# Second projections of the MLP and of the gated stage: half the outputs by seven products of blocks in place of eight

## The chip, the cores and the metric

One core of one Trainium2 chip. The metric is the device time of one execution in microseconds. The core has TensorE (PE, matrix products), VectorE (DVE), ScalarE (ACT), GpSimd (POOL) and SyncE (SP, which here issues the loads).

## The reference

Two decoder blocks run on 256 tokens of width 1024, in float32. The parts that matter here are the feed-forward stages at the end of each block:

```python
h = rmsnorm(x, norm_mlp[layer])
x = x + jnp.square(jax.nn.relu(h @ w_up[layer])) @ w_down[layer]      # w_up 1024x4096, w_down 4096x1024
...
g, u = jnp.split(n @ w_ffn_in, 2, axis=-1)                            # w_ffn_in 1024x5632
return (jax.nn.silu(g) * u) @ w_ffn_out                               # w_ffn_out 2816x1024
```

The rest (two kinds of attention, retention, a state-space mixer, gated linear attention) lies before the MLP, between the two stages, and around them, and the change does not touch it.

## The kernel before

**Numbers in two parts.** Every float32 factor is split in a rounded part `h` (fp32r) and the rest `l`. A product of two such factors is three matmuls, `h h`, `h l` and `l h`. ACT makes `h` by a rounding copy (`round_tile`, L1040), DVE makes `l = raw - h` by a TENSOR_TENSOR with both inputs in SBUF (`rest_of_tile`, L1561).

**Weights.** They come as tiles of 128x1024 (512 KB). SP loads tile i into one of `RAW` = 4 slots (`raws`), once tile i-4 has its `l` (semaphore `lo`, L2391). ACT may round tile i into one of `PARTS` = 5 pairs of slots (`parts`) once TensorE has released tile i-5. The functions `until` and `full` place these roundings and rests, at build time, between the other work of ACT and DVE: before an instruction that waits for a matmul, all those whose slot is released earlier. Each engine then keeps to its order.

**The two stages.** `mlp(u, n, up, w_down)` builds both: u = 0 is the MLP (n = 16 blocks of 256 hidden columns), u = 1 the gated stage (n = 11). Block q of the hidden layer comes from `up(q)`, by `fm`: two tiles and 48 matmuls of 256 columns in the MLP (L374 to L376), four tiles and 96 in the gated stage (`gate` and `prod`). DVE and ACT make it the activated block, in fp32 in `tmps[q % 4]` (MLP: relu on ACT L1300, times itself on DVE L1601; gated: gate scaled on DVE, silu on ACT L1514, product on DVE), and its two parts in `ups[q % 4]` (ACT, then DVE L1595). Then `down(q, 0)` and `down(q, 1)` add the block's share to output columns 0 to 511 and 512 to 1023 of both groups of 128 tokens: one weight tile and 12 matmuls of 512 columns each (L738 to L740). TensorE runs `up(q)`, `down(q-2, 0)`, `down(q-2, 1)`, `up(q+1)` and so on. The four sums stay in four PSUM banks over the stage, and four banks are left for the rest. Some `down(q, 1)` are kept for the end, so that the outputs of columns 0 to 511 can be added to `x` (`residual`), and turned for the next stage, under them.

**GpSimd** computes only small things, the reciprocal roots of the norms, between long waits.

## Time and profile before

| | |
|---|---|
| median of 3 runs | 962.2 us (961.87 to 962.92) |
| profiled execution | 961.55 us, of it span 959.5 us |
| TensorE busy | 952.3 us, 99% |
| VectorE busy | 635.0 us, 66% |
| ScalarE busy | 520.4 us, 54% |
| GpSimd busy | 62.9 us, 7% |
| loads | 170 MB, 178 GB/s in the mean |

The span is the profiled part of an execution. Matmuls overlap in TensorE, so a row's duration is longer than the step from one matmul to the next. What one costs is read from the starts.

### The profile page before, as it was taken

How to read it: one execution, taken by the hardware profiler on the slowest of the kernel's cores; microseconds unless marked ns; L12 is line 12 of the kernel's file. 1: busy time of each engine (PE TensorE's matmuls, PEld its weight loads, DVE VectorE, ACT ScalarE, POOL GpSimd, SP SyncE). 2: the span in 40 equal slices, each digit the busy share in tenths (PEclk: the TensorE clock that was granted, in tenths of full speed). 3: DMA queues.
4: the chain of work that ended last, by engine and by line, in shares of the span. 5: the costliest groups of instructions: out<-in, count | busy, mean ns of one | idle time of the engine just before them, and what ended most of it. 6: DMA issues, size and time to landing. Idle time of an engine off the chain costs nothing.

```text
span 959.5 us, 16218 instructions
## 1 busy us (share of the span) xinstructions
PE 952.3 (99%) x6674; PEld 862.3 (90%) x6674; DVE 635.0 (66%) x826; ACT 520.4 (54%) x788; POOL 62.9 (7%) x112
## 2 busy tenths in 40 slices
PE   9999999999999999999999999999999999999997
PEld 7877889989998888989987999998998899999996
DVE  5768685777555555778867787786666466555545
ACT  5577554555444544666865674545455445444443
POOL 3100001001000000324000001100000010000000
PEclk9999999999999999999999999999999999999999
DMA  9974536556665666556564465555655347565661
GB/s 307 316 231 129 152 88 177 155 176 191 206 196 176 189 185 181 158 181 193 151 198 146 119 180 194 161 191 171 195 163 172 114 154 220 182 202 171 196 192 47
DMA packets 133546, 170.39 MB, mean 178 GB/s; under 512 B 5825, under 2 KB 97297, under 8 KB 133473
## 3 DMA queue, kind: packets, MB, share of 16 engines
q1 hardware_dynamic: 131408, 165.07, 55.7%
q10 hardware_dynamic: 1424, 2.84, 0.9%
q0 software_dynamic: 640, 1.44, 0.6%
q8 instruction: 53, 0.87, 0.4%
q14 instruction: 21, 0.16, 0.1%
HBM read 168.28 MB, written 1.05 MB: 176 GB/s over the span
## 4 chain that ended last, share of the span: by engine, by line
PE 98%; DVE 1%; issue 0%; ACT 0%; POOLq 0%; POOL 0%; ACTq 0%
PE ps L374 15%; PE ps L375 15%; PE ps L376 15%; PE ps L405 8%; PE ps L406 8%; PE ps L407 8%; PE ps L739 5%; PE ps L740 5%; PE ps L738 5%; PE ps L357 4%; PE ps L461 3%; PE ps L494 1%; PE ps L492 1%; PE ps L493 1%; PE ps L627 1%; PE ps L660 1%
## 5 line engine op out<-in xcount | busy, mean ns | idle before, releaser
L1561 DVE TENSOR_TENSOR parts<-raws,parts 128x1024 fp32r<-128x1024 f32 (+2 forms) x307 | 367.3, 1213 | 217.7 <-ACT parts L1040 216.9
L1040 ACT ACTIVATE parts<-raws 128x1024 fp32r<-128x1024 f32 (+2 forms) x307 | 315.5, 1045 | 235.2 <-PE ps L376 133.5
L374 PE MATMUL ps<-room_r,parts 128*128 128x256 f32 x1248 | 351.9, 282 | 0.0
L375 PE MATMUL ps<-room_r,parts 128*128 128x256 f32 x1248 | 348.6, 279 | 0.0
L376 PE MATMUL ps<-room_r,parts 128*128 128x256 f32 x1248 | 348.2, 279 | 0.0
L374 PEld LDWEIGHTS ps<-room_r,parts 128*128 128x128 f32 x1248 | 234.6, 188 | 5.8 <-issue 4.3
L375 PEld LDWEIGHTS ps<-room_r,parts 128*128 128x128 f32 x1248 | 234.7, 188 | 1.3
L376 PEld LDWEIGHTS ps<-room_r,parts 128*128 128x128 f32 x1248 | 234.6, 188 | 0.0
L405 PE MATMUL ps<-parts,room_r 128*128 128x512 f32 (+1 forms) x336 | 133.9, 399 | 0.4 <-DVE parts L1561 0.4
L407 PE MATMUL ps<-parts,room_r 128*128 128x512 f32 (+1 forms) x336 | 131.1, 390 | 0.0
L406 PE MATMUL ps<-parts,room_r 128*128 128x512 f32 (+1 forms) x336 | 131.1, 390 | 0.0
L738 PE MATMUL ps<-parts,room_r 128*128 128x512 f32 x204 | 80.7, 396 | 0.0
L740 PE MATMUL ps<-parts,room_r 128*128 128x512 f32 x204 | 80.7, 396 | 0.0
L739 PE MATMUL ps<-parts,room_r 128*128 128x512 f32 x204 | 80.7, 396 | 0.0
L405 PEld LDWEIGHTS ps<-parts,room_r 128*128 128x128 f32 x336 | 63.1, 188 | 16.1 <-issue 1.7
L407 PEld LDWEIGHTS ps<-parts,room_r 128*128 128x128 f32 x336 | 63.1, 188 | 14.4
L406 PEld LDWEIGHTS ps<-parts,room_r 128*128 128x128 f32 x336 | 63.2, 188 | 13.4 <-issue 0.5
L1595 DVE TENSOR_TENSOR room_r<-room,room_r 128x512 fp32r<-128x512 f32 x47 | 32.5, 692 | 32.5 <-ACT room_r L1305 11.9
L740 PEld LDWEIGHTS ps<-parts,room_r 128*128 128x128 f32 x204 | 38.3, 188 | 9.2
L739 PEld LDWEIGHTS ps<-parts,room_r 128*128 128x128 f32 x204 | 38.3, 188 | 8.2
L738 PEld LDWEIGHTS ps<-parts,room_r 128*128 128x128 f32 x204 | 38.3, 188 | 8.2
L1595 DVE TENSOR_TENSOR room<-room 128x256 f32<-128x256 f32 (+6 forms) x85 | 37.5, 474 | 2.3 <-ACT room L1392 0.7
(225 smaller groups left out, 878.5 us busy)
## 6 DMA issues: line engine op xcount, KB each, us to landing
raws<-in_w_in SPq DMA_DIRECT2D x99, 512.0 KB, 4.5
raws<-in_w_ffn_in SPq DMA_DIRECT2D x44, 512.0 KB, 4.2
raws<-in_w_up SPq DMA_DIRECT2D x32, 512.0 KB, 4.2
raws<-in_w_down SPq DMA_DIRECT2D x32, 512.0 KB, 4.4
raws<-in_w_ffn_out SPq DMA_DIRECT2D x22, 512.0 KB, 4.2
raws<-in_w_xkv SPq DMA_DIRECT2D x16, 512.0 KB, 4.4
raws<-in_w_out SPq DMA_DIRECT2D x8, 512.0 KB, 4.5
raws<-in_w_up_ssd SPq DMA_DIRECT2D x8, 512.0 KB, 5.9
```

Of the source, the lines that this page charges most:

```text
L374: e.matmul(ps, wh, hT[0][:, k, :], start=k == 0, stop=False)
L375: e.matmul(ps, wh, hT[1][:, k, :], start=False, stop=False)
L376: last = e.matmul(ps, wl, hT[0][:, k, :], start=False, stop=k == K - 1)
L405: e.matmul(ps, hT[0][:, k, tok], wh, start=k == 0, stop=False)
L406: e.matmul(ps, hT[0][:, k, tok], wl, start=False, stop=False)
L407: last = e.matmul(ps, hT[1][:, k, tok], wh, start=False, stop=k == K - 1)
L738: e.matmul(ps, uh[:, k, tok], wh, start=q == 0 and k == 0, stop=False)
L739: e.matmul(ps, uh[:, k, tok], wl, start=False, stop=False)
L740: last = e.matmul(ps, ul[:, k, tok], wh, start=False, stop=q == n - 1 and k == 1)
L1040: e.activation(t.h, t.raw, ACT.Copy).then_inc(s["hi"], 1)
L1561: e.tensor_tensor(t.l, t.raw, t.h.bitcast(F32), ALU.subtract).then_inc(s["lo"], 1)
L1595: return e.tensor_tensor(o, i0, i1, op)
```

## The change

Output columns 0 to 511 of both second projections are computed by a scheme of the Strassen and Winograd kind. Per block q, the activations are four blocks of 128x128 (two token groups by two halves of the 256 hidden columns), the weights four blocks of 128x256. Eight block products become seven, each of three matmuls of 256 columns, 21 in place of 12 of 512 columns (`down_by_sums`). They need four sums or differences of the blocks on either side: of the activations (`up_sums_of`, into `u_sums`, 128x512 values) and of the weights (`sums_of`, into `w_sums`, 128x1024 values). GpSimd makes both by three TENSOR_TENSOR each (for the last block DVE makes those of the activations). The weights' sums are a tile of their own in the ring of `parts` (`weight_sums`), which ACT rounds and DVE takes the rest of, so block q has one tile more. Only 768 of 1024 columns of the loaded tile still need that. The activations' sums are rounded by ACT (`sums_rounded`) and have their rest from DVE (`sums_rest`). A raw slot is free once `lo` and the sums are done. At the end the seven products, which lie in four banks, are combined by DVE (`join`). Six banks are now held over the stage, two are left for `up`. In the MLP four `down(q, 1)` are kept for the end, where there were three.

```diff
+            def weight_sums(of):
+                i = len(tiles)
+                h, l = (parts[:, i % PARTS, j, 0:TILE].rearrange("p (k n) -> p k n", k=4) for j in range(2))
+                t = Tile(i, [], 4, 256, chunks(w_sums[len(made) % 2], 4), h, l)
+                t.sums, of.sums = of, t
+                of.raw, of.h, of.l = (v.rearrange("p k (f n) -> p (k f) n", f=2)[:, 1:4, :] for v in (of.raw, of.h, of.l))
+                tiles.append(t)
+                made.append(t)
+                t.nth_sums = len(made)
                 return t
...
-                own = [bank() for _ in range(4)]
+                by_sums = u in (0,1)
+                products = [bank() for _ in range(4)] if by_sums else None
+                own = [None] * 2 * by_sums + [bank() for _ in range(2 if by_sums else 4)]
+                late = 4 if by_sums and u == 0 else 3
+                def product(at, left, right, first, last_):
+                    ps = psum[:, products[at // 2], 256 * (at % 2):256 * (at % 2) + 256]
+                    for (lh, rh), begins, over in (((0, 0), first, False), ((0, 1), False, False), ((1, 0), False, last_)):
+                        last = e.matmul(ps, left[lh], right[rh], start=begins, stop=over)
+                    return last
+                def down_by_sums(q):
+                    need(s["upT"], (16 if u else 0) + q + 1)
+                    w_ = weight(w_down[256 * q:256 * q + 256, 0:512], 2, 512)
+                    sums = weight_sums(w_)
+                    u11, u21, u12, u22 = ([v[:, k, t * P:t * P + P] for v in ups[q % 4]] for k in range(2) for t in range(2))
+                    s3, s1, s2, s4 = ([v[:, i, :] for v in us[q % 4]] for i in range(4))
+                    w11, w22, w21 = ([v[:, i, :] for v in (w_.h, w_.l)] for i in range(3))
+                    t1, t3, t2, t4 = ([v[:, i, :] for v in (sums.h, sums.l)] for i in range(4))
+                    begins, over = q == 0, q == n - 1
+                    need(s["lo"], w_.i + 1)
+                    product(0, u11, w11, begins, False)
+                    last = product(1, u12, w21, False, over)
+                    if over:
+                        ends(last, ("product", u, 0), products[0])
+                    need(s["usT"], nth_us[u] + q + 1)
+                    w_.release = done(product(4, s4, w22, begins, False))
+                    need(s["lo"], sums.i + 1)
+                    product(2, s2, t2, begins, False)
+                    last = product(3, s1, t1, False, over)
+                    if over:
+                        ends(last, ("product", u, 1), products[1])
+                    last = product(5, s3, t3, False, over)
+                    if over:
+                        ends(last, ("product", u, 2), products[2])
+                    last = product(6, u22, t4, begins, over)
+                    if over:
+                        ends(last, ("product", u, 3), products[3])
+                        sums.release = count
+                    else:
+                        sums.release = done(last)
                 def down(q, h):
+                    if by_sums and h == 0:
+                        return down_by_sums(q)
...
                 for q in range(2, n):
                     up(q)
                     down(q - 2, 0)
-                    if q < n - 1:
+                    if q - 2 < n - late:
                         down(q - 2, 1)
                 down(n - 2, 0)
                 down(n - 1, 0)
                 if u:
                     return last_outputs([(q, weight(w_down[256 * q:256 * q + 256, 512:D], 2, 512)) for q in range(n - 3, n)],
                                         own, n)
-                down(n - 3, 1)
+                for q in range(n - late, n - 2):
+                    down(q, 1)
                 if u == 0:
                     where["tail", MIX2] = Group(None, count, None)
                     for t in range(2):
-                        out_of((("down", u), 0, t))
+                        if by_sums:
+                            need(s["joined"], t + 1)
+                        else:
+                            out_of((("down", u), 0, t))
                         turn_x(MIX2, t, 0)
                 down(n - 2, 1)
                 down(n - 1, 1)
...
                 t = tiles[hi]
-                e.wait_ge(landed[t.slot], t.load)
+                if t.nth_sums:
+                    e.wait_ge(s["w_sums"], t.nth_sums)
+                else:
+                    e.wait_ge(landed[t.slot], t.load)
...
+            def sums_rounded(u, q, n):
+                if q == n - 1:
+                    e.wait_ge(s["last_u_sums"], 1 + (u and 1))
+                else:
+                    e.wait_ge(s["u_sums"], nth_us[u] - (u and 1) + q + 1)
+                e.activation(us[q % 4][0], chunks(u_sums[q % 2], 4), ACT.Copy).then_inc(s["us_hi"], 1)
+            def first_copied(u):
+                full(("product", u, 0))
+                e.activation(first_product, psum[:, where["product", u, 0].bank, 0:256], ACT.Copy).then_inc(s["first_product"], 1)
             def up(q):
+                until(where["up", q].at)
+                if q:
+                    sums_rounded(0, q - 1, 16)
                 full(("up", q))
...
+            def up_sums_of(u, q, sem):
+                v, o = tmps[q % 4].rearrange("p k (t n) -> p (k t) n", t=2), chunks(u_sums[q % 2], 4)
+                if nth_us[u] + q >= 2:
+                    e.wait_ge(s["usT"], nth_us[u] + q - 1)
+                step(e.tensor_tensor(o[:, 0:2, :], v[:, 0:4:3, :], bc(v[:, 1, :], 1, [P, 2, P]), ALU.subtract))
+                settle()
+                step(e.tensor_tensor(o[:, 2, :], o[:, 1, :], v[:, 0, :], ALU.add))
+                settle()
+                e.tensor_tensor(o[:, 3, :], o[:, 2, :], v[:, 2, :], ALU.subtract).then_inc(s[sem], 1)
+            def sums_rest(u, q):
+                rest(chunks(u_sums[q % 2], 4), us[q % 4], "us_hi", nth_us[u] + q + 1, "usT")
+            def join(u, factor):
+                p = [psum[:, where["product", u, at // 2].bank, 256 * (at % 2):256 * (at % 2) + 256] for at in range(7)]
+                p37 = chunks(psum[:, where["product", u, 2].bank, :], 2)
+                c = slice(0, 512)
+                until(where["product", u, 3].at)
+                e.wait_ge(s["pe"], where["product", u, 1].at)
+                e.wait_ge(s["first_product"], nth_joint[u] + 1)
+                step(tt(joint[:, 0, :], p[2], first_product, ALU.subtract))
+                settle()
+                emptied(tt(joint[:, 1, :], joint[:, 0, :], p[3], ALU.subtract), ("product", u, 1))
+                emptied(tt(joined[:, 0, 256:512], p[1], first_product, ALU.add), ("product", u, 0))
+                out_of(("product", u, 1))
+                e.wait_ge(s["pe"], where["product", u, 2].at)
+                step(tt(joined[:, :, 0:256], bc(joint[:, 1, :], 1, [P, 2, 256]), p37, ALU.subtract))
+                settle()
+                out_of(("product", u, 0))
+                stt(x[:, 0, c], joined[:, 0, :], factor[0], x[:, 0, c], ALU.mult, ALU.add).then_inc(s["joined"], 1)
+                emptied(tt(joint[:, 1, :], p[5], joint[:, 0, :], ALU.subtract), ("product", u, 2))
+                out_of(("product", u, 2))
+                e.wait_ge(s["pe"], where["product", u, 3].at)
+                emptied(tt(joined[:, 1, 256:512], joint[:, 1, :], p[6], ALU.add), ("product", u, 3))
+                out_of(("product", u, 3))
+                stt(x[:, 1, c], joined[:, 1, :], factor[1], x[:, 1, c], ALU.mult, ALU.add).then_inc(s["joined"], 1)
...
             for q in range(11):
                 r, name = tmps[q % 4], ("gate", q)
+                until(where[name].at)
+                if q:
+                    sums_rest(1, q - 1)
                 full(name)
                 emptied(tt(r, halves(bank_of(name)), rows_of(2), ALU.mult), name)
                 name = ("prod", q)
                 full(name)
                 e.wait_ge(s["gated"], q + 1)
                 emptied(tt(r, halves(bank_of(name)), r, ALU.mult), name)
+                if q == 10:
+                    out_of(name)
+                    up_sums_of(1, q, "last_u_sums")
                 rest(r, ups[q % 4], "up_hi", 16 + q + 1, "upT")
+            sums_rest(1, 10)
...
+            def sums_of(t):
+                raw, o = chunks(raws[:, t.slot, :], 4), t.sums.raw
+                e.wait_ge(landed[t.slot], t.load)
+                if t.sums.nth_sums > 2:
+                    e.wait_ge(s["lo"], made[t.sums.nth_sums - 3].i + 1)
+                step(e.tensor_tensor(o[:, 0:2, :], raw[:, 1:3, :], bc(raw[:, 0, :], 1, [P, 2, 256]), ALU.add))
+                settle()
+                step(e.tensor_tensor(o[:, 2, :], o[:, 0, :], raw[:, 2, :], ALU.add))
+                settle()
+                e.tensor_tensor(o[:, 3, :], o[:, 2, :], raw[:, 3, :], ALU.add).then_inc(s["w_sums"], 1)
+            def sums(u, n, ahead=0):
+                for q in range(ahead):
+                    sums_of(made[nth_us[u] + q].sums)
+                for q in range(n):
+                    if q < n - 1:
+                        name = ("prod" if u else "up", q)
+                        e.wait_ge(taken[where[name].bank], where[name].use)
+                        up_sums_of(u, q, "u_sums")
+                    if q >= ahead:
+                        sums_of(made[nth_us[u] + q].sums)
...
-            for t in tiles:
-                if t.i >= RAW:
-                    before = tiles[t.i - RAW]
-                    e.wait_ge(s["lo"], before.i + 1)
+            for t in loaded:
+                if t.before:
+                    e.wait_ge(s["lo"], t.before.i + 1)
+                    if t.before.sums:
+                        e.wait_ge(s["w_sums"], t.before.sums.nth_sums)
                 for to, v in t.srcs:
                     e.dma_start(to, v).then_inc(landed[t.slot], 16)
```

Place one: VectorE over one block of the gated stage (`parts` are the weights' parts; `room` with `rows_rstd` is the scaled gate; `room` with `s_gated` the product; `room_r` with `s_up_hi` the rest of the activated block). Before:

```order
L1595 TENSOR_TENSOR room<-ps,rows_rstd 128x512 [waits s_pe]
L1561 TENSOR_TENSOR parts<-raws,parts 128x1024 [waits s_hi] x2
L1595 TENSOR_TENSOR room<-ps,room 128x512 [waits s_gated,s_pe]
L1595 TENSOR_TENSOR room_r<-room,room_r 128x512 [waits s_up_hi]
L1561 TENSOR_TENSOR parts<-raws,parts 128x1024 [waits s_hi] x4
```

The same place after, where `s_us_hi` stands for the rounded sums of the activations of the block before:

```order
L1698 TENSOR_TENSOR room_r<-room,room_r 128x512 [waits s_us_hi]
L1698 TENSOR_TENSOR room<-ps,rows_rstd 128x512 [waits s_pe]
L1664 TENSOR_TENSOR parts<-raws,parts 128x1024 [waits s_hi] x2
L1698 TENSOR_TENSOR room<-ps,room 128x512 [waits s_gated,s_pe]
L1698 TENSOR_TENSOR room_r<-room,room_r 128x512 [waits s_up_hi]
L1664 TENSOR_TENSOR parts<-raws,parts 128x1024 [waits s_hi] x3
L1664 TENSOR_TENSOR parts<-raws,parts 128x768 [waits s_hi]
L1664 TENSOR_TENSOR parts<-room,parts 128x1024 [waits s_hi]
```

A rest of 128x512 that waits for GpSimd's sums now stands ahead of the gate, and the rest of the weights' sums (`parts<-room,parts`) behind the loaded tiles.

Place two: GpSimd over one block of the gated stage, none of which was there before (`room<-room` are the activations' sums, those with `raws` the weights'):

```order
L2449 TENSOR_TENSOR room<-raws 128x512 [waits s_lo,s_landed3]
L2451 TENSOR_TENSOR room<-room,raws 128x256 [waits s_pool_step]
L2453 TENSOR_TENSOR room<-room,raws 128x256 [waits s_pool_step]
L2437 TENSOR_TENSOR room<-room 128x256 [waits s_usT,s_taken7]
L2439 TENSOR_TENSOR room<-room 128x128 [waits s_pool_step]
L2441 TENSOR_TENSOR room<-room 128x128 [waits s_pool_step]
```

Each instruction waits for the one ahead of it, and the activations' sums of block q+1 stand behind the weights' sums of block q, whose tile is loaded behind the four tiles of `up(q+2)`.

Place three: ScalarE before the last block of the MLP (`room<-ps` is the relu of that block). Before:

```order
L1040 ACTIVATE parts<-raws 128x1024 [waits s_pe,s_landed3]
L1040 ACTIVATE parts<-raws 128x1024 [waits s_pe,s_landed0]
L1040 ACTIVATE parts<-raws 128x1024 [waits s_pe,s_landed1]
L1040 ACTIVATE parts<-raws 128x1024 [waits s_pe,s_landed2]
L1300 ACTIVATE room<-ps 128x512 [waits s_pe]
L1305 ACTIVATE room_r<-room 128x512 [waits s_taken6,s_pe]
```

After:

```order
L1116 ACTIVATE parts<-raws 128x768 [waits s_pe,s_landed2]
L1116 ACTIVATE parts<-room 128x1024 [waits s_pe,s_w_sums]
L1116 ACTIVATE parts<-raws 128x768 [waits s_pe,s_landed3]
L1116 ACTIVATE parts<-room 128x1024 [waits s_pe,s_w_sums]
L1380 ACTIVATE room_r<-room 128x512 [waits s_u_sums]
L1393 ACTIVATE room<-ps 128x512 [waits s_pe]
L1398 ACTIVATE room_r<-room 128x512 [waits s_taken5,s_pe]
L1380 ACTIVATE room_r<-room 128x512 [waits s_last_u_sums]
```

Two roundings that wait for GpSimd's weight sums, of blocks 13 and 14, now stand ahead of the relu of block 15.

## Rows read from the trace of the kernel before

**Rows 1.** The page: busy time and instructions of engines, TensorE's clock, chain

```profile
PE 952.3 (99%) x6674; PEld 862.3 (90%) x6674; DVE 635.0 (66%) x826; ACT 520.4 (54%) x788; POOL 62.9 (7%) x112
...
PEclk9999999999999999999999999999999999999999
...
PE 98%; DVE 1%; issue 0%; ACT 0%; POOLq 0%; POOL 0%; ACTq 0%
```

**Rows 2.** Waits of TensorE, whole span: us in total, times, longest

```profile
PE ps L357 <- DVE junk L1688: 1.0, 1, 1.0
PE ps L405 <- DVE parts L1561: 0.4, 1, 0.4
```

**Rows 3.** Timeline of TensorE in the MLP: start us, duration us, instruction

```profile
301.12 0.40 PE L740 MATMUL ps<-parts,room_r 128*128 128x512 f32 x1
...
303.92 0.40 PE L740 MATMUL ps<-parts,room_r 128*128 128x512 f32 x1
304.15 0.28 PE L374 MATMUL ps<-room_r,parts 128*128 128x256 f32 x1
...
308.36 0.28 PE L374 MATMUL ps<-room_r,parts 128*128 128x256 f32 x1
```

**Rows 4.** Timeline of VectorE, one block of the MLP (x2: two merged)

```profile
310.85 0.68 DVE L1601 SCALAR_TENSOR_TENSOR room<-ps,room 128x512 f32<-128x512 f32 x1
312.29 0.69 DVE L1595 TENSOR_TENSOR room_r<-room,room_r 128x512 fp32r<-128x512 f32 x1 [0.76 <-ACT room_r L1305]
313.25 2.36 DVE L1561 TENSOR_TENSOR parts<-raws,parts 128x1024 fp32r<-128x1024 f32 x2 [0.26 <-ACT parts L1040]
316.70 1.23 DVE L1561 TENSOR_TENSOR parts<-raws,parts 128x1024 fp32r<-128x1024 f32 x1 [1.10 <-ACT parts L1040]
```

**Rows 5.** Timeline of ScalarE, the same block

```profile
309.95 0.60 ACT L1300 ACTIVATE room<-ps 128x512 f32<-128x512 f32 x1 [0.27 <-PE ps L376]
311.63 0.63 ACT L1305 ACTIVATE room_r<-room 128x512 fp32r<-128x512 f32 x1 [1.07 <-DVE room L1601]
315.61 1.06 ACT L1040 ACTIVATE parts<-raws 128x1024 fp32r<-128x1024 f32 x1 [1.45 <-PE ps L740]
```

**Rows 6.** Timeline of VectorE, gated stage: a tile's rest, then the gate

```profile
863.99 1.23 DVE L1561 TENSOR_TENSOR parts<-raws,parts 128x1024 fp32r<-128x1024 f32 x1 [2.98 <-ACT parts L1040]
865.13 0.68 DVE L1595 TENSOR_TENSOR room<-ps,rows_rstd 128x512 f32<-128x512 f32 x1
```

**Rows 7.** GpSimd's instructions by line: duration ns min/median/max, first and last start us

```profile
L2307 POOL TENSOR_TENSOR ssq<-ssq x2: 191/192/194, 223.6 to 223.7; 128x1 f32<-128x1 f32 x2
L2339 POOL TENSOR_TENSOR room<-room x7: 254/275/1030, 443.9 to 449.4; 128x32 f32<-128x32 f32 x7
```

**Rows 8.** Timelines of GpSimd and VectorE before the MLP, then GpSimd with VectorE idle

```profile
219.19 1.42 POOL L2264 TENSOR_SCALAR ssq<-ssq 128x1 f32<-128x1 f32 x1 [61.12 <-ACT junk L1085]
220.69 1.39 POOL L2257 TENSOR_TENSOR ssq<-ssq,half 128x1 f32<-128x1 f32 x1
218.16 4.63 DVE L1561 TENSOR_TENSOR parts<-raws,parts 128x1024 fp32r<-128x1024 f32 x4
...
670.87 0.30 POOL L2264 TENSOR_SCALAR ssq<-ssq 128x1 f32<-128x1 f32 x1
671.25 0.56 POOL L2257 TENSOR_TENSOR ssq<-ssq,half 128x1 f32<-128x1 f32 x1
```

**Rows 9.** Timelines of both where GpSimd reads 32 columns

```profile
448.18 1.14 POOL L2337 TENSOR_SCALAR room<-room 128x32 f32<-128x32 f32 x1
449.41 1.03 POOL L2339 TENSOR_TENSOR room<-room 128x32 f32<-128x32 f32 x1
447.91 4.76 DVE L1561 TENSOR_TENSOR parts<-raws,parts 128x1024 fp32r<-128x1024 f32 x4
```

**Rows 10.** The page's loads: count, KB each, median us from issue to landing

```profile
raws<-in_w_down SPq DMA_DIRECT2D x32, 512.0 KB, 4.4
raws<-in_w_ffn_out SPq DMA_DIRECT2D x22, 512.0 KB, 4.2
```

94 lines of the change are left out of this document (68 added, 26 removed).

## The prediction

> **What bounds the kernel now.** I read the page first: TensorE is busy in 99% of the span, runs at its full level (granted clock 9 of 9 in all slices, 2.4 GHz) and fills 98% of the chain that ended last [rows 1]. Then its waits: 1.4 us in the whole span [rows 2]. So the kernel ends earlier only by fewer TensorE columns, and every wait that TensorE gets is added in full. The price of a column: 12 matmuls of 512 columns lie between the starts 301.12 and 303.92, 0.2333 us each; 36 of 256 columns between 304.15 and 308.36, 0.117 us each, just half [rows 3]. Last, what the helpers have free: per block of the MLP, TensorE needs 48 x 0.117 + 24 x 0.2333 = 11.2 us, VectorE 4 x 1.13 (two merged rests take 2.36, one 1.23, so a step is 1.13) + 0.6 + 0.6 = 5.7 us [rows 4], ScalarE less.
>
> **What the change takes away.** Per block 12 matmuls of 512 columns (2.80 us) become 21 of 256 (2.45 us): 0.35 us, for 16 + 11 blocks 9.45 us. An MLP block then needs 10.85 us, a gated one 96 x 0.117 + 2.45 + 2.80 = 16.45 us. I take the step of 0.117 for the products too, since those of rows 3 change weights as often. If nothing waited, that would be all.
>
> **What it adds, and what hides it.** ScalarE gets a rounding of 1024 columns (1.06 us) and one of 512 (0.63) [rows 5], VectorE a rest of each (1.13 and 0.60), less a quarter of one tile's. VectorE's two-input work in an MLP block is then 4 x 1.13 + 0.85 + 2 x 0.60 = 6.6 us of 10.85. That alone is hidden by TensorE.
>
> GpSimd's price is bounded from rows: an add or product of 1 column takes 0.19 us, of 32 columns 0.254 at least [rows 7], so 0.0021 us per column: 1.24 us for 512, 0.72 for 256, 0.45 for 128. The weights' sums are 1.24 + 0.72 + 0.72, with 0.1 us between dependent ones 3.0 us; the activations' 0.72 + 0.45 + 0.45, 1.9 us. No row is wider than 32 columns for two inputs, so this is an estimate; the lower end is VectorE's own 1.13 us per 1024 columns, the upper the 32-column median (0.275, 0.0027 per column). Together 4.9 us per block: hidden too, if GpSimd ran freely.
>
> **It does not run freely.** While VectorE takes four rests back to back, an instruction of GpSimd that takes 0.30 us elsewhere takes 1.42, and one of 0.56 takes 1.39 [rows 8]. They end 0.2 to 0.5 us behind a boundary between two rests (218.16 + 2 x 1.13 = 220.4 against 220.6; 221.6 against 222.1). So GpSimd waits for the end of a VectorE instruction with two SBUF inputs, and comes in at the next boundary. The other way round: four rests take 4.63 us with one-column work beside them, 4.76 with two instructions of 32 columns beside them [rows 8, 9], about 0.0021 x 32 for each. VectorE seems to wait while GpSimd reads. That wait is shown for 0.1 us only; here it would be 0.3 to 1.1 us at a time. I take it as shown. The Trainium skill (SBUF — State Buffer, Who interferes with whom) states it as a rule: a VectorE instruction with two SBUF inputs and a GpSimd instruction that reads SBUF exclude each other, and the second blocks fully; by it the waits below stand as I sum them, without it the first rival holds. The Trainium skill (GPSIMD Engine Reference, Elementwise — side-by-side cycle accounting) gives 4497 ns for an add of 2048 columns, about 0.0022 per column.
>
> **Gated stage: a loop longer than TensorE's 16.45 us.** VectorE's gate of block q+2 stands behind the rest of the activations' sums of block q+1; GpSimd makes those behind the weights' sums of block q; these wait for that tile to land; its load waits for a rest that stands behind the last gate. One turn of the loop: load 4.2 [rows 10]; GpSimd 3.0 and 1.9; ScalarE's rounding 0.63; VectorE's rest 0.60, gate 0.68 [rows 6]; silu 0.5 (as a relu) and rounding 1.06 on ScalarE [rows 5]; two rests 1.13 + 1.23, the second of which frees the slot; some 0.3 for semaphores: 15.2 us. That would be hidden. GpSimd's waits: the first sum finds VectorE in a rest (1.0), the second behind the 768-column rest that came in between (0.8), the last behind the rest of the weights' sums (1.0): 2.8 us. The loop is 18.0, over TensorE by 1.5; I take 1.4. Tiles made ahead absorb it at first (ScalarE rounds a tile some 8 us before its use); for some 6 of the last blocks it is a wait, 8.4 us. At the end blocks 8, 9 and 10 give three seven-product groups in a row, 2.45 us of TensorE each, while GpSimd and VectorE need some 4 us for each: 2 x 1.5 = 3.0 us more. Stage: 11.4 of waits.
>
> **MLP.** Shared by turns, VectorE's 6.6 and GpSimd's 1536 x 0.0021 = 3.2 us fill 9.8 of 10.85 us; the steady part just holds, with 1.4 us at its start, where the ring is short. At the end ScalarE must round the weight sums of block 14 ahead of the relu of block 15. From the end of `up(14)`: relu applied and bank free 3.4 (0.3 + 0.6 + 0.6 and the turns behind GpSimd), activation sums 2.9 with one wait, wait for a rest 1.0, weight sums 3.4, rounding 1.06, next rounding 0.5, VectorE's rest of the one and of the other 1.9: 14.2 us. TensorE asks for it after 2.45 + 5.6 + 2.45 + 0.7 = 11.2 us: a wait of 3.0. The tile of block 15 has its rest only behind the relu, three sums on VectorE and two rests, 4.0 us on, and is asked for after 1.8: 2.2. The tile after it is loaded into the same slot (4.4), then rounded and rested before `join` starts, and `join` is late for the turns under 5.6 us of cover: 1.9 more. Stage: 1.4 + 7.1 = 8.5.
>
> **Moved, at no price.** Two banks are left for `up` where four were; a bank is emptied within some 3 us and asked for again a block later (10.85 or more). If that cover went, each block would wait. In the last stage `join` (some 4.5 us) lies under 8.4 us of `last_outputs`.
>
> **Sum** against the profiled execution's 961.55 us (span 959.5 and 2.05 around it): 961.55 - 9.45 + 11.4 + 8.5 = 972.0. The median of runs is 0.65 above that execution, so **972.7 us**.
>
> **Rivals.** *VectorE is not held by long GpSimd reads, or hardly.* For: only 0.13 us of such delay is in the trace [rows 9]. The waits fall below the 1.25 us that the gated loop has to spare, that stage waits 0.4, the MLP only at its end 3.3 to 4.7: 962.2 - 9.45 + 4.4 = 957. It decides at 1.25 us of waits per turn. *Everything is hidden*, the rings absorb the ends too: 962.2 - 9.45 = 953; against it, the chains at the MLP's end are over the cover even with short waits. *The column on GpSimd costs 0.0025 or more*: per block its reads grow by 1536 x 0.0004 = 0.6 us, with VectorE's work 10.4 of 10.85 us and with the fixed parts over it; some 0.8 us more for seven gated blocks and 0.4 for fourteen of the MLP: 984. *The change does not do what it says*: should matmuls of 256 columns with new weights each time step slower than 0.133 (2.80/21), the products cost more than before; rows 3 speak against it, 0.117.
>
> **Chances.** Forecast, 965 to 979: 0.54. Longer, above 979: 0.11. First rival, 955 to 960: 0.22. All hidden, 951 to 955: 0.08. Between, 960.3 to 964: 0.05. Range 955 to 981, leaving out the hidden case and the tail. 0.2% (1.9 us) is what a measurement here can tell from no change. Faster 0.31, same 0.04, slower 0.65.
>
> **What would show it.** TensorE's busy time 9 to 10 us lower, with waits of some 20 us, for `parts` rests and the sums' rests: about 1.4 us per block from the fourth gated block on, most of the MLP's in its last 30 us. GpSimd's 512-column add at 1.2 us alone and up to 2.4 beside rests; VectorE's rests of 1.23 us now up to 2.4. Wrong if rests stay at 1.23 beside GpSimd's adds, if the gated block stays at 16.5 us, or if GpSimd's column is much cheaper than 0.0021.

## The result: 23.7 us slower, in the direction of the forecast and far outside its size

The changed kernel takes **985.73 us** (median of 4 runs, 984.57 to 985.97) against 962.04 us of the kernel before (961.79 to 962.92): ratio 1.0243, 95% interval 1.0231 to 1.0255. Forecast were 972.7 us, range 955 to 981. The profiled execution took 985.97 us, its span is 984.2 us.

The page of the changed kernel (busy time, TensorE's granted clock in 40 slices, shares of the chain that ended last), to be read against [rows 1]:

```profile
PE 954.7 (97%) x6917; PEld 874.8 (89%) x6917; DVE 716.1 (73%) x898; ACT 554.3 (56%) x844; POOL 245.5 (25%) x268
...
PEclk9999999999999998999999999999999999999999
...
PE 78%; DVE 7%; DMA 5%; POOL 4%; ACT 3%; issue 2%; POOLq 0%; ACTq 0%; DVEq 0%
```

TensorE's busy time rose by 2.4 us, although its work shrank: a busy TensorE is not one at full speed. Slice 16 (about 370 to 390 us) shows a lowered clock, and a fifth of the chain now runs over VectorE, loads, GpSimd and ScalarE. TensorE's waits of more than 0.2 us (engine and line, whom it waited for: total, times, longest), against [rows 2]:

```profile
PE ps L762 <- DVE parts L1664: 5.6, 4, 2.6
PE ps L807 <- DVE parts L1664: 4.1, 7, 0.7
PE ps L399 <- DVE parts L1664: 3.9, 7, 2.3
PE ps L762 <- DVE room_r L1698: 2.8, 1, 2.8
PE ps L399 <- DVE room L1698: 2.0, 1, 2.0
PE ps L430 <- DVE parts L1664: 1.1, 1, 1.1
PE ps L382 <- DVE junk L1833: 1.0, 1, 1.0
PE ps L399 <- DVE room L1704: 0.9, 1, 0.9
```

Without the two at L430 and L382, which lie outside the two stages, that is 19.3 us, all behind VectorE: rests of tiles (`parts`), the rest of the activations' sums (`room_r`) and a bank not yet empty (`room`). The forecast was 19.9 us of waits. So the list seems to say that all came as foreseen; the time says otherwise. Where the rest is, the timelines tell. TensorE's timeline (start, duration) has three marks that both kernels pass: the turn of `x` behind the MLP (its transposition for the next stage, by a product with `ident`), the last matmul, and the end of the span (959.5 and 984.2). Before:

```profile
394.61 0.60 PE L461 MATMUL ps<-ident,x 128*128 128x128 f32 x4
953.57 0.28 PE L780 MATMUL ps<-parts,room_r 128*128 128x256 f32 x1
```

After:

```profile
403.20 0.66 PE L486 MATMUL ps<-ident,x 128*128 128x128 f32 x4 [0.22 <-DVE x L1704]
976.28 0.28 PE L853 MATMUL ps<-parts,room_r 128*128 128x256 f32 x1
```

To the turn 8.6 us were lost, from there to the last matmul 14.1, behind it 2.0 (5.9 us became 7.9). And the products themselves, the 21 of one block in one row of the same timeline:

```profile
269.77 0.28 PE L401 MATMUL ps<-room_r,parts 128*128 128x256 f32 x1
269.88 2.65 PE L762 MATMUL ps<-parts,room_r 128*128 128x256 f32 x21
272.37 0.39 PE L807 MATMUL ps<-parts,room_r 128*128 128x512 f32 x1
```

From start to start 272.37 - 269.88 = 2.49 us for 21 products, 0.1186 each, where 2.80 us stood before. An undisturbed block of the MLP takes 10.89 us (before 11.20), a gated one 16.49 (before 16.80): 0.31 us of gain, not 0.35.

With that, each stretch can be set against its term of the forecast; products saved are added back, so that each row shows what was lost there. The starts of the first projections mark the blocks: 238.40 and 253.39 us in the MLP (before, the first of them at 236.96), then ten blocks of 10.90; 820.44 to 944.03 in the gated stage (before, the first at 808.03).

| term, us | forecast | measured | how measured |
|---|---|---|---|
| products, 27 blocks | -9.45 | -8.4 | 27 x 0.31 |
| MLP, start | +1.4 | +5.9 | 238.40 - 236.96 + 0.31, and 14.99 - 10.89 |
| MLP, middle | 0 | 0 | 10.90 a block |
| MLP, end and join | +7.1 | +7.7 | 8.6 + 16 x 0.31 - 5.9 |
| gated, start | 0 | +4.1 | (820.44 - 403.20) - (808.03 - 394.61) + 0.31 |
| gated, loop | +8.4 | +8.2 | 123.59 us for 7 blocks, - 7 x 16.49 |
| gated, end | +3.0 | +5.2 | 14.1 + 11 x 0.31 - 4.1 - 8.2 |
| behind the last matmul | 0 | +2.0 | 7.9 - 5.9 |
| sum | +10.45 | +24.7 | spans: 984.2 - 959.5 = 24.7 |

The starts, 8.6 us over their terms, are most of the miss. Behind three of TensorE's long waits (2.3 us at 242, 2.8 at 382 and 2.0 at 802) the granted clock fell as well, from its level of 2.4 GHz to that of 1.2 GHz; behind the one of 2.6 us at 965 it stayed at 1.00. Windows of the changed kernel (stretch, length, busy time and instructions of PE, PEld, DVE, ACT, POOL, then granted clock, DMA share, GB/s):

```profile
240.00:242.00 2.00, 0.00 (x0) 0.00 (x0) 1.75 (x2) 2.00 (x3) 1.92 (x2) 1.00 0.18 63
242.00:244.00 2.00, 1.75 (x12) 1.75 (x13) 2.00 (x3) 1.39 (x2) 1.57 (x2) 0.86 0.21 45
244.00:246.00 2.00, 2.00 (x11) 2.00 (x11) 1.86 (x2) 0.00 (x0) 0.00 (x0) 0.50 1.06 332
246.00:248.00 2.00, 2.00 (x16) 2.00 (x16) 0.04 (x1) 1.13 (x2) 0.00 (x0) 0.78 0.73 243
...
384.00:388.00 4.00, 2.37 (x12) 2.11 (x11) 3.76 (x5) 4.00 (x5) 0.00 (x0) 0.50 0.11 13
...
804.00:806.00 2.00, 2.00 (x12) 2.00 (x11) 2.00 (x2) 0.70 (x1) 0.00 (x0) 0.50 0.00 0
```

TensorE stood still from 239.98 to 242.25; behind that the row of 244 to 246 us counts 11 matmuls, where the same 2 us of e6 below, at the full level, have 20. No step of the prediction had this.

### The profile page after: what moved, and what is told of

It reads as the page before. It is cut to its first block, busy times and chain, and to the rows that moved or that the text cites. A ratio compares the mean times of both kernels' runs of the same rounds, so it can differ in the third digit from the quotient of the medians.

```text
span 984.2 us, 17100 instructions
## 1 busy us (share of the span) xinstructions
PE 954.7 (97%) x6917; PEld 874.8 (89%) x6917; DVE 716.1 (73%) x898; ACT 554.3 (56%) x844; POOL 245.5 (25%) x268
## 3 DMA queue, kind: packets, MB, share of 16 engines
q0 software_dynamic: 640, 1.44, 0.6%
## 4 chain that ended last, share of the span: by engine, by line
PE 78%; DVE 7%; DMA 5%; POOL 4%; ACT 3%; issue 2%; POOLq 0%; ACTq 0%; DVEq 0%
PE ps L399 12%; PE ps L400 12%; PE ps L401 12%; PE ps L430 8%; PE ps L431 8%; PE ps L432 8%; PE ps L382 4%; DVE parts L1664 4%; PE ps L762 4%; DMA raws<-in_w_ffn_out 3%; PE ps L486 3%; ACT parts L1116 2%; DVE room L1698 1%; POOL room L2449 1%; PE ps L808 1%
## 5 line engine op out<-in xcount | busy, mean ns | idle before, releaser
L1664 DVE TENSOR_TENSOR parts<-raws,parts 128x1024 fp32r<-128x1024 f32 (+3 forms) x307 | 381.7, 1266 | 131.3 <-ACT parts L1116 130.2
L1116 ACT ACTIVATE parts<-raws 128x1024 fp32r<-128x1024 f32 (+3 forms) x307 | 308.1, 1026 | 164.8 <-PE ps L401 87.8
L399 PEld LDWEIGHTS ps<-room_r,parts 128*128 128x128 f32 x1248 | 236.0, 189 | 14.3 <-issue 7.5
L430 PE MATMUL ps<-parts,room_r 128*128 128x512 f32 (+1 forms) x336 | 133.9, 399 | 1.1 <-DVE parts L1664 1.1
L1698 DVE TENSOR_TENSOR room_r<-room,room_r 128x512 fp32r<-128x512 f32 x74 | 59.8, 809 | 42.2 <-ACT room_r L1398 11.2
L762 PE MATMUL ps<-parts,room_r 128*128 128x256 f32 x567 | 74.4, 287 | 8.4 <-DVE parts L1664 5.6
L762 PEld LDWEIGHTS ps<-parts,room_r 128*128 128x128 f32 x567 | 71.1, 194 | 9.5 <-issue 6.0
L430 PEld LDWEIGHTS ps<-parts,room_r 128*128 128x128 f32 x336 | 63.1, 188 | 16.9 <-DVE parts L1664 2.0
L2449 POOL TENSOR_TENSOR room<-raws 128x512 f32<-128x512 f32 x27 | 45.6, 1688 | 125.7 <-DMA raws<-in_w_ffn_out 88.5
L432 PEld LDWEIGHTS ps<-parts,room_r 128*128 128x128 f32 x336 | 63.1, 188 | 14.4
L431 PEld LDWEIGHTS ps<-parts,room_r 128*128 128x128 f32 x336 | 63.2, 188 | 13.4 <-issue 0.5
L2422 POOL TENSOR_SCALAR ssq<-ssq 128x1 f32<-128x1 f32 x10 | 6.4, 639 | 252.4 <-ACT junk L1161 252.1
L1664 DVE TENSOR_TENSOR parts<-room,parts 128x1024 fp32r<-128x1024 f32 x27 | 36.6, 1354 | 24.5 <-ACT parts L1116 24.5
L1116 ACT ACTIVATE parts<-room 128x1024 fp32r<-128x1024 f32 x27 | 28.5, 1057 | 38.0 <-POOL room L2453 33.2
```

The source lines that it names most:

```text
L399: e.matmul(ps, wh, hT[0][:, k, :], start=k == 0, stop=False)
L430: e.matmul(ps, hT[0][:, k, tok], wh, start=k == 0, stop=False)
L431: e.matmul(ps, hT[0][:, k, tok], wl, start=False, stop=False)
L432: last = e.matmul(ps, hT[1][:, k, tok], wh, start=False, stop=k == K - 1)
L762: last = e.matmul(ps, left[lh], right[rh], start=begins, stop=over)
L1116: e.activation(t.h, t.raw, ACT.Copy).then_inc(s["hi"], 1)
```

## Experiments

Theory 1: GpSimd and VectorE keep each other from the SBUF, so the stages turn on a chain of both, and the waits that follow also lower the clock. Theory 2: the products, the added rounding, the fifth tile in the ring and the join cost the time, whoever adds. Theory 3: VectorE is never held, GpSimd's own latency is late. The kernel before took 961.7 to 962.1 us beside each group of runs.

| run | us (range) | ratio to before, 95% interval |
|---|---|---|
| e1 VectorE makes the sums | 967.48 (967.27 to 968.03) | 1.0059, 1.0042 to 1.0076 |
| e2 MLP alone | 970.4 (969.4 to 970.81) | 1.0086, 1.0071 to 1.0101 |
| e3 gated stage alone | 977.05 (976.11 to 977.42) | 1.0155, 1.014 to 1.017 |
| e4 sums of one column | 962.46 (961.5 to 964.24) | 1.0009, 1.0 to 1.0018 |
| e5 e1 and idle adds on GpSimd | 1017.79 (1017.52 to 1018.06) | 1.0582, 1.0563 to 1.0601 |
| e6 zeros in the waits | 987.98 (986.71 to 988.66) | 1.027, 1.0256 to 1.0285 |
| e7 order of the tail | 984.41 (984.22 to 984.78) | 1.0235, 1.0221 to 1.0249 |
| e8 four repairs | 968.7 (966.32 to 969.9) | 1.0068, 1.0055 to 1.0082 |
| e9 VectorE makes the activations' sums | 977.65 (976.72 to 978.65) | 1.0163, 1.0147 to 1.0178 |
| e10 last blocks by eight products | 961.05 (960.0 to 962.45) | 0.9992, 0.9983 to 1.0 |
| e11 gated stage alone, repaired | 963.4 (962.66 to 964.61) | 1.0016, 1.0007 to 1.0025 |
| e12 e10 with cover for the join | 959.14 (958.54 to 959.46) | 0.9969, 0.9958 to 0.998 |
| e13 e12 with GpSimd's sums | 974.79 (973.38 to 976.17) | 1.0132, 1.0118 to 1.0146 |

**e1, who adds.** VectorE calls the same functions; GpSimd's calls go.

```diff
 def rest_of_tile():
...
     t = tiles[lo]
+    if t.sums:
+        if not t.nth_sums:
+            sums_of(t)
     e.wait_ge(s["hi"], lo + 1)
...
-    if q == 15:
-        out_of(name)
-        up_sums_of(0, q, "last_u_sums")
+    out_of(name)
+    up_sums_of(0, q, "last_u_sums" if q == 15 else "u_sums")
...
-sums(0, 16, 1)
```

Expected: 

> VectorE makes all sums that GpSimd made (each block's activation sums right after the product, each weight tile's sums ahead of that tile's rest); TensorE's program is that of the changed kernel. Theory 1 (GpSimd and VectorE keep each other from the SBUF, so the stages turn on a chain of the two, and the waits that this makes also lower TensorE's clock): the sums cost VectorE about 2 us of a block in place of 4.9 us of GpSimd, the gated loop falls below TensorE's 16.45 us, and the time is 953 to 960 us. Theory 2 (the seven products themselves, the added rounding, the fifth tile of the ring and the join cost the time, whoever adds): over 975 us. Theory 3 (VectorE was never held, only GpSimd's own latency is late): 953 to 960 us as well, so this run doesn't part theories 1 and 3.

967.48 us: 18.3 of the 23.7 us hang on GpSimd, and theory 2 is out as the main cause. But 967 is 7 us above the band: something is left that no GpSimd explains. Its own wait list has 5.2 us for `parts` at L762, 3.6 of them in one wait at 381.58 us, at the end of the MLP; its middle blocks take 10.89 and 16.49 us, undisturbed. There VectorE is busy 79.5 of 87 us (265 to 352 us, eight blocks): 9.9 of 10.9 us a block, with nothing left to catch up with once the last seven-product groups follow each other.

**e2 and e3, the two stages.** `by_sums = u in (0,)` and `u in (1,)`, with the helpers' loops of the other stage as before.

Expected: 

> Seven products in the MLP alone, the gated stage as before. Theory 1: the MLP's part of the loss as read from the two traces, +8.6 us to the first turn behind it, so 969 to 972 us; the granted clock falls to 0.50 around 244 and 385 us again. Theory 2 (costs in proportion to the blocks, 16 of 27): 14 of 23.7 us, 976 us. If the clock is lowered by something other than the two waits there, it stays at 1.00 in this run or falls elsewhere.

Expected: 

> Seven products in the gated stage alone, the MLP as before. Theory 1: +13.8 us to the last product and +2.0 us behind it, so 976 to 979 us, with a gated loop of 17.9 us in the middle. Theory 2 (11 of 27 blocks, and one join of two): +9.7 us, 972 us.

970.4 and 977.05 us, both in theory 1's bands: 8.6 and 15.3 us over their group's 961.78, together 23.9 where the change has 23.7. The losses add up; they don't share blocks in proportion to 16 and 11. In e2 the clock is lowered at the MLP's end again (0.57 in 382 to 386 us), but not in 242 to 248, although the wait there is as long (2.29 us at 242.72, against 2.27 in the changed kernel).

**e4, nearly free sums.** GpSimd's adds shrink to one column of each chunk, and the rest of the sums is left out, in the style of

```diff
-step(e.tensor_tensor(o[:, 2, :], o[:, 0, :], raw[:, 2, :], ALU.add))
+step(e.tensor_tensor(o[:, 2, 0:1], o[:, 0, 0:1], raw[:, 2, 0:1], ALU.add))
```

Expected: 

> The changed kernel, but each of GpSimd's six operations of a block takes one column of each chunk (the rest of the sums is left out and stays zero): the same waits and signals, nearly no time of GpSimd on the SBUF. Theories 1 and 3: all waits of TensorE over 1 us in the two stages but the first of each go, the clock stays at 1.00, the time is 952 to 958 us. Theory 2: over 975 us. If e1 is slower than this one, the difference is what VectorE's own adding costs.

962.46 us, above the band of 952 to 958. So GpSimd's time is worth 23.3 us, yet **with sums that cost nearly nothing the change gains nothing**: the 8.4 us that the products save are eaten by its own structure. Its timeline has them: 0.4 + 0.7 + 1.2 us of delays in the MLP, 2.1 at the turns (`join` late), 0.9 and 0.6 in the gated stage, 2.0 behind the last matmul.

**e5, is VectorE held?** The kernel of e1, and GpSimd makes adds of the same shapes on scratch data; nobody waits for them.

```diff
+for q in range(n - 1):
...
+    e.wait_ge(taken[where[name].bank], where[name].use)
...
+    step(e.tensor_tensor(v[:, 0:2, :], b[:, 0:4:3, :], bc(b[:, 1, :], 1, [P, 2, P]), ALU.subtract))
...
+    step(e.tensor_tensor(o[:, 3, :], o[:, 2, :], a[:, 3, :], ALU.add))
```

Expected: 

> The kernel of e1 (VectorE makes all sums, 967.48 us), and GpSimd makes, once a block, six additions of the same shapes as the sums on scratch data of its own, for which nobody waits. Theory 1 (the two engines keep each other from the SBUF): VectorE is busy 9.9 us of the MLP's 10.85 us block in e1 and 13.2 of 16.45 in the gated stage; 4.4 us of GpSimd a block, where they can't lie beside VectorE's, lengthen the MLP's block to 12.5 to 14 us and the time to 990 to 1020 us; VectorE's rests of 1024 columns show a mean well above 1.23 us. Theory 3 (VectorE is never held): 967 us, within 1 us of e1, and rests of 1.23 us.

1017.79 us, 50 us over e1. VectorE's weight sums (128 x 512, then twice 128 x 256: count, busy us, mean ns, idle before) in e1, undisturbed:

```profile
L1666 DVE TENSOR_TENSOR room<-raws 128x512 f32<-128x512 f32 x27 | 18.5, 686 | 0.7 <-DMA raws<-in_w_down 0.7
L1668 DVE TENSOR_TENSOR room<-room,raws 128x256 f32<-128x256 f32 x27 | 11.5, 425 | 0.9
```

and in e5, with GpSimd's 512-column add under them:

```profile
L1666 DVE TENSOR_TENSOR room<-raws 128x512 f32<-128x512 f32 x27 | 35.5, 1314 | 0.3 <-DMA raws<-in_w_down 0.3
L1668 DVE TENSOR_TENSOR room<-room,raws 128x256 f32<-128x256 f32 x27 | 18.2, 674 | 0.9
...
L2492 POOL TENSOR_TENSOR room<-room 128x512 f32<-128x512 f32 x25 | 49.6, 1985 | 2.0
```

The same instruction of the same shape takes 1314 ns in place of 686, and VectorE waits for nothing that these adds make. Theory 3 and the prediction's first rival are refuted: **VectorE is held**, and GpSimd too (1985 ns for an add that takes 1.28 us alone). The MLP's block is 13.03 us long, the gated one 17.95. The Trainium skill (SBUF — State Buffer, Who interferes with whom) has the rule that the prediction leaned on: a VectorE instruction with two SBUF inputs and a GpSimd instruction that reads the SBUF exclude each other. This run agrees with it in both directions.

**e6, does the clock cost?** TensorE multiplies zeros where it would wait.

```diff
+    def keep(n, alone=False):
...
+        for _ in range(n):
+            e.matmul(psum[:, products[3], 256:384], nothing, nothing, start=alone, stop=alone)
...
+                    if q == n - 2 and not u:
+                        keep(10)
                     need(s["usT"], nth_us[u] + q + 1)
```

Expected: 

> The changed kernel, but TensorE multiplies a block of zeros (8, 10, 6, 8 and 10 times, into an unused half bank) ahead of five of its waits: the one at 242 us, the two around 380 us, the one at 802 us and the one at 965 us. They lie in time in which it would wait; about 0.2 us each. Theory 1, second part (the waits of 2 to 3 us lower the granted clock, and that adds to the loss): the granted clock stays at 1.00 around 245 and 385 us and the time falls by 4 to 8 us from 985.7, to 978 to 982 us. Rival (the clock of 0.50 there costs little because TensorE waits for VectorE in those stretches anyway): 984 to 988 us, with the waits shorter and the same ends.

987.98 us: no gain, 2.3 us more. The clock did stay up, windows of e6:

```profile
244.00:246.00 2.00, 2.00 (x20) 2.00 (x19) 1.98 (x2) 0.47 (x1) 0.00 (x0) 1.00 1.06 327
...
384.00:388.00 4.00, 3.00 (x26) 3.03 (x27) 4.00 (x4) 3.82 (x5) 0.00 (x0) 1.00 0.40 129
```

TensorE came to the mark behind the wait at 242 us 1.4 us sooner (251.96 us against 253.39), and the turn behind the MLP still stood at 403.33 (403.20 in the changed kernel). At the MLP's end e6 waits for VectorE's adds into `x` (0.4, 0.9 and 0.5 us ahead of its turns, where the changed kernel waits 0.2), so there the lead is lost. The second part of theory 1 falls: the lowered clock did not add to the time behind the MLP. How much the zeros themselves cost isn't separated; they are 42 matmuls, and 8 of them fill 1.7 us (238.50 to 240.20).

**e7, the tail.** The last quarter's add and squares move ahead of row 0's product.

```diff
-e.wait_ge(s["rstd"], 2 * nth_rstd["final"] + 1)
...
-stt(x[:, 0, 512:D], x[:, 0, 512:D], rstd[sq_of["final"]][0], gain[:, 512:D], ...)
...
 tt(big[:, 1, 512:768], part, gain[:, 512:768], ALU.mult).then_inc(s["last_row"], 1)
 full("last")
 emptied(stt(rest_, bank_of("last")[:, 0:256], ...), "last")
...
 e.tensor_tensor_reduce(junk[:, 768:D], rest_, rest_, 1 / D, ...)
+e.wait_ge(s["rstd"], 2 * nth_rstd["final"] + 1)
...
+stt(x[:, 0, 512:D], x[:, 0, 512:D], rstd[sq_of["final"]][0], gain[:, 512:D], ...)
```

Expected: 

> The changed kernel, but in VectorE's last stretch the add of the last quarter of columns and its squares stand ahead of the product of row 0, which waits for GpSimd's root. Theory 1, third part (the late join pushes the last adds behind that product, so the time from the last matmul to the end is 7.9 us in place of 5.9): 983.5 to 984.5 us, the end 6.2 to 6.9 us behind the last matmul. Rival (the end hangs on the output's transfer or on GpSimd's root, not on the order): within 0.3 us of 985.7.

984.41 us, 1.3 us less. VectorE's timeline in the changed kernel, where the last matmul starts at 976.28:

```profile
974.97 1.41 DVE L1704 SCALAR_TENSOR_TENSOR x<-ps,ssq,x 128x512 f32<-128x512 f32 x2
977.59 0.75 DVE L1704 SCALAR_TENSOR_TENSOR x<-x,ssq,rows 128x512 f32<-128x512 f32 x1 [1.22 <-POOL ssq L2566]
978.26 0.42 DVE L1698 TENSOR_TENSOR big<-x,rows 128x256 f32<-128x256 f32 x1
978.60 0.48 DVE L1704 SCALAR_TENSOR_TENSOR x<-ps,ssq,x 128x256 f32<-128x256 f32 x1
```

The add at 978.60 could have begun at some 976.5; it stands behind a product that waits for a root, which the late `join` (VectorE at work without a gap from 969.68) has pushed to 977.59. In e7 the add starts at 976.53, right behind its matmul.

**e8, four repairs.** e1, the banks taken behind `up(2)`, the tail of e7, and at the end of the MLP (with a like order in the gated stage)

```diff
-down(n - 2, 0)
-down(n - 1, 0)
+for q, h in ((14, 0), (12, 1), (15, 0), (13, 1), (14, 1)):
+    down(q, h)
```

Expected: 

> Four repairs together: VectorE makes the sums (as in e1), the eight banks of the products are taken behind the third block's first projection in place of ahead of it, the second-half groups of the last blocks stand between the seven-product groups at the end of both stages, and the tail is that of e7. From e1's 967.5 us: 1.1 and 0.8 us of waits for a bank go, 1.3 to 2.0 us of the tail, and of the 5 us of waits and 1.9 us of lowered clock at the MLP's end about half: 959 to 962 us. If the MLP's end doesn't yield (VectorE 9.9 us of 10.85 us has nothing left to catch up with), 962 to 964 us.

968.7 us, a miss: no better than e1. Its second turn stands at 399.06 with a wait of 2.89 us for VectorE; e1's is at 398.46. Spreading TensorE's groups moved the wait and left VectorE's work as it was, and VectorE is still what ends last there.

**e9, the dose.** VectorE makes the activations' sums, GpSimd keeps the weights'.

Expected: 

> The changed kernel, but VectorE makes the activations' sums (three adds, about 1.0 us a block by e1's rows of 425, 292 and 292 ns); GpSimd keeps the weights' sums (1.28 + 0.74 + 0.74 us a block alone). Theory 1 (a chain of load, GpSimd and VectorE turns the gated stage in 17.9 us): GpSimd's 1.7 to 1.9 us of activations' sums leave the chain and 1.0 us of VectorE comes in its place, so the gated loop is at or just under TensorE's 16.45 us, about 8 to 9 us of waits there go, and the time is 973 to 978 us. Theory 3 (only GpSimd's latency for the activations' sums is late, VectorE isn't held): the same gain, but VectorE's rests of 1024 columns stay at 1.23 us beside GpSimd's adds.

977.65 us, in the band: 8.1 us less for 1.7 us less of GpSimd's adding per block. VectorE's rests of 768 columns still take 1313 ns in the mean (952 in e1), which speaks against theory 3. The gated block is 16.49 us for three blocks, then 16.6 to 17.1. In the MLP a block now takes 11.1 in place of 10.9 us: VectorE has taken on work and is still held.

**e10, spare VectorE at the ends.** As e1 with late banks and e7's tail, and blocks 14, 15 and 9, 10 go by eight products into the two banks that the first projections leave; `join` begins two blocks sooner.

```diff
-if by_sums and h == 0:
+if by_sums and h == 0 and q < m:
     return down_by_sums(q)
+if by_sums and h == 0 and q == m:
+    own[0], own[1] = bank(), bank()
```

Expected: 

> VectorE makes the sums, the banks are taken late and the tail is that of e7, and the last two blocks of each stage (14, 15 and 9, 10) have eight products in place of seven, in the two banks that the first projections leave. So the seven products end two blocks earlier, the join lies beside the last two blocks, and VectorE is spared about 4 us a block at the end of the MLP, where e1 and e8 show it to be the engine waited for. If VectorE's work at the end is what is left of the loss (3.6 + 1.3 us of waits and 2 us of lowered clock in the MLP, 1.9 us in the gated stage, 2 us behind the last matmul): 23 blocks give 8.05 us, some 1.5 us stay lost: 954 to 957 us, faster than both. If something else held the ends of e1: 962 us or more.

961.05 us, 6.4 less than e1, though short of the band. The waits of 1.1 and 3.6 us at e1's MLP end are gone; left is one of 1.97 us at the turn, with a clock of 0.58 behind it, where only one second-half group (2.8 us) stands between block 15 and the first turn; e12 tests that.

**e11, the gated stage alone, repaired.**

Expected: 

> Seven products in the gated stage alone, VectorE makes the sums, banks taken late, the tail of e7. In the gated stage VectorE is busy 13.2 of 16.45 us a block in e1, so its loop is TensorE's: 11 blocks give 3.85 us, the last block's wait takes 0.9 us, the start 0.4, the tail 0 to 1: 959 to 961 us. If VectorE's adding holds TensorE there too: 963 us or more.

963.4 us, at the upper case: 11 x 0.31 = 3.4 us are won, 1.6 us lost at the first second-half tile of the stage, 2.3 at block 10 and 1.1 behind the last matmul (961.4 - 954.35 = 7.05 us, against 5.9). VectorE's adding holds TensorE at both ends even where its middle is free (92.65 of 116 us busy in e1's gated stage).

**e12, cover for the join.** `late = 4` for the MLP in e10.

Expected: 

> e10 with one change: at the end of the MLP the second-half group of block 12 waits for its turn too, so that two second-half groups (5.6 us) in place of one stand between block 15 and the first turn. In e10 TensorE waited 1.97 us for the join there and then had a granted clock of 0.58 in 388 to 392 us. If the join is what is late: both go, and the 961.05 us of e10 become 957 to 959 us. If VectorE's rests of those tiles are late instead: within 1 us of e10.

**959.14 us**, ratio 0.9969 (0.9958 to 0.998), the one version that beats both kernels. All of TensorE's waits in it over 0.2 us:

```profile
PE ps L430 <- DVE parts L1684: 1.2, 1, 1.2
PE ps L382 <- DVE junk L1857: 1.0, 1, 1.0
PE ps L814 <- DVE parts L1684: 1.0, 1, 1.0
PE ps L486 <- DVE x L1724: 0.7, 1, 0.7
PE ps L399 <- DVE parts L1684: 0.6, 2, 0.4
```

23 blocks give 7.1 us; 3.0 us arrive.

**e13, GpSimd again.** e12 with `sums(0, 14, 1)` and `sums(1, 9)` on GpSimd.

Expected: 

> e12, but GpSimd makes the sums again, as in the changed kernel. All that the others repaired stays repaired (banks late, last two blocks of each stage by eight products, tail, cover of the join), so the difference to e12 is GpSimd's price alone. Theory 1: the gated loop turns in 17.9 us again over some six blocks (8 to 9 us), the MLP's first blocks lose 3 to 5 us as before, the MLP's end and the gated end little: 968 to 974 us. Rival (with the ends repaired GpSimd's sums are hidden): within 3 us of e12.

974.79 us, 15.7 over e12 and just above theory 1's band; the rival (hidden) is out. It shows where GpSimd's price lies with the ends repaired. The MLP's start takes 5.9 us again (waits ahead of 235.48 and 242.24, 15.01 us for the block in which e12 takes 11.59), although no bank is waited for. And in the gated stage every block is long from the first on: 17.90, 17.92, 17.93, 17.94, 17.95, 17.92, 17.93 us. Of the seven turns between its marks, none is absorbed by tiles made ahead. Ahead of the first mark e13 loses 1.6 us, but e12 loses 1.3 there too; so in the gated stage GpSimd's price is the loop, 7 x 1.44 us, and not its start.

## Why the prediction was off: the mechanism held, its starts did not

- **The direction and the mechanism** were right. GpSimd's adds take 1.28, 0.74 and 0.46 us alone (forecast 1.24, 0.72, 0.45). VectorE's rests, 1.23 us before, are held up to 2.07 us beside them (e5 shows the holding where VectorE waits for nothing of GpSimd's). Both engines in one gated turn of the changed kernel, GpSimd first:

```profile
856.99 2.19 POOL L2449 TENSOR_TENSOR room<-raws 128x512 f32<-128x512 f32 x1 [10.85 <-DMA raws<-in_w_ffn_out]
859.26 1.33 POOL L2451 TENSOR_TENSOR room<-room,raws 128x256 f32<-128x256 f32 x1
860.67 0.73 POOL L2453 TENSOR_TENSOR room<-room,raws 128x256 f32<-128x256 f32 x1
861.36 0.74 POOL L2437 TENSOR_TENSOR room<-room 128x256 f32<-128x256 f32 x1
862.18 0.46 POOL L2439 TENSOR_TENSOR room<-room 128x128 f32<-128x128 f32 x1
862.72 1.36 POOL L2441 TENSOR_TENSOR room<-room 128x128 f32<-128x128 f32 x1
...
855.68 4.32 DVE L1664 TENSOR_TENSOR parts<-raws,parts 128x1024 fp32r<-128x1024 f32 x3
862.53 1.23 DVE L1664 TENSOR_TENSOR parts<-room,parts 128x1024 fp32r<-128x1024 f32 x1 [2.53 <-ACT parts L1116]
864.78 0.69 DVE L1698 TENSOR_TENSOR room_r<-room,room_r 128x512 fp32r<-128x512 f32 x1 [1.02 <-ACT room_r L1380]
865.39 0.68 DVE L1698 TENSOR_TENSOR room<-ps,rows_rstd 128x512 f32<-128x512 f32 x1
```

  Three of GpSimd's six adds find VectorE in a rest, at 0.9, 0.6 and 0.9 us over their price: 2.4 us in the three places for which the prediction gave 2.8 (1.0, 0.8, 1.0). From gate to gate (847.45 to 865.39) the turn takes 17.94 us, forecast 18.0. No run takes away the holding alone, so that the loop would be hidden without it (15.2 us) stays the prediction's sum.
- **The step that failed is what the prediction let the ring hide at the starts**: "tiles made ahead absorb it at first" in the gated stage, and 1.4 us for the MLP's start, a figure with no sum behind it. The prediction let the gated loop cost six blocks of 1.4 us, 8.4 in all. Start and loop together cost 12.3 us (4.1 ahead of the first mark, 8.2 behind it), and the MLP's start took 5.9. In the changed kernel's own trace the first turns do look absorbed (16.49 and 17.10 us, then 17.93 to 18.23), but the lead was paid for ahead of the first mark, where TensorE waited 2.0 us for a bank. e7, the same program up to its tail, splits it otherwise: 1.9 us ahead of the mark, 9.1 behind it.
- **GpSimd's sums are the cause**, by e12 against e13: the MLP's start loses 0.7 us with VectorE's sums and 5.9 with GpSimd's, the gated start and loop 1.3 + 0.5 = 1.8 against 1.6 + 7 x 1.44 = 11.7. e13 has no waits for a bank and loses much the same as the changed kernel, so these waits (0.9 us at 226.81, 2.0 at 802.33), which the prediction had "at no price", are mostly where the lateness shows. Of the MLP's 5.9 us, 1.4 are the lowered clock, by e6, which gained them there and lost them at the MLP's end. How the MLP's start gets late, ahead of the wait at 242.25 us:

```profile
235.71 2.27 POOL L2449 TENSOR_TENSOR room<-raws 128x512 f32<-128x512 f32 x1
236.76 1.77 DVE L1698 TENSOR_TENSOR room_r<-room,room_r 128x512 fp32r<-128x512 f32 x1
239.17 0.63 ACT L1398 ACTIVATE room_r<-room 128x512 fp32r<-128x512 f32 x1 [2.26 <-DVE room L1704]
240.78 2.54 DVE L1664 TENSOR_TENSOR parts<-raws,parts 128x1024 fp32r<-128x1024 f32 x2 [0.25 <-ACT parts L1116]
```

  VectorE's rest of the activations' sums is held by GpSimd's add (1.77 us in place of 0.69), the activated block behind it comes late, ScalarE stands idle 2.26 us for it, with the roundings of the next tiles behind it in its order, and TensorE needs the rest of the first of them. The prediction had such a chain for the MLP's end and none for its start.
- **The gated stage's end** was sized at 3.0 and took 5.2 us: the waits of 1.1, 0.3 and 2.6 us in the products of blocks 9 and 10, 0.5 in the first projection of block 10, and 0.7 of slower steps behind the waits. The MLP's end and join, 7.1, came to 7.7.
- **The join at the end of the kernel** was put under `last_outputs` at no price; it fits there, but pushes VectorE's last adds behind a wait for a root: 2.0 us, of which e7's order gets 1.3 back.
- **The products** save 0.31 us, not 0.35: 21 of them take 2.49 us, while the step of 0.117 that was taken from the first projections gives 2.45. That is 1.1 us over 27 blocks. The rival that asked for a step above 0.133 is out, as is that of a GpSimd column of 0.0025: (1.28 - 0.74) / 256 is 0.0021.
- **"That alone is hidden by TensorE"**, said of VectorE's work, held in the middle of the stages only. Starts, ends and tail cost 9 us (962.46 - 961.78 + 8.4) in e4, where GpSimd adds next to nothing, and 14 us (967.48 - 961.78 + 8.4) in e1, where VectorE adds; the prediction's first rival, the case without the holding, allowed 4.4. What of the 7.7 us at the MLP's end is GpSimd's and what VectorE's own share isn't separated to the tenth, since the two work in one chain.

That the waits listed by the profile (19.3 us) match the forecast (19.9) is luck: they are partly other waits (2.9 us are for banks), and behind many of them comes a slower first step or a lowered clock, which the list doesn't count. The marks on the timeline give the 33.1 us (24.7 and the 8.4 saved) that the table's losses sum to.

## What to carry to other kernels

Work moved to GpSimd isn't free beside a VectorE that reads two SBUF operands. As an estimate, add both engines' time as if they were one: in e5 9.9 + 4.4 = 14.3 us for an MLP block that took 13.03, and 13.2 + 4.4 = 17.6 for a gated one that took 17.95. Here VectorE did the same sums in about half the time (2.5 us a block against GpSimd's 4.4 alone), and moving them there was worth 18.3 us. A helper that was busy in 91% of the block of the engine that sets the pace (VectorE in e1's MLP) kept up in the middle and fell behind at the end, where the seven-product groups follow each other. Leaving the last blocks in the old form puts backlog and join beside them: e10 and e12 together are 8.3 us under e1, of which part is e7's order and the late banks; e8, which had these two without the old form, gained nothing. A loop longer than that of the engine that sets the pace cost here from nearly its first turn on; don't credit the ring with absorbing it, unless its lead is seen in the trace.

## What the hardware showed beyond that

The granted clock stood at 0.50 (1.2 GHz) in 244 to 246 us, behind a TensorE wait of 2.27 us that ended at 242.25, and was back at 1.00 in 248 to 250; likewise in 804 to 806 us behind the wait that ended at 802.33. Near 384 us it was 0.50 for 6 us, with a second wait among them. The length of the wait doesn't settle it: behind 2.29 us at 242.72 in e2 and 2.58 us at 965.36 in the changed kernel it stayed at 1.00. Why isn't shown. Held up with zeros (e6), it gained nothing here.

Adds of one column on GpSimd (e4) that stand beside rests took 0.45 to 0.68 us in the mean, with a minimum of 0.19; those of the activations' sums, where VectorE was less in the way, took 0.23. So a narrow add beside rests costs mostly waiting, not columns.
